# One ring of weights for projection and scan, four turned token tiles, and another order of ScalarE's copies in the scan of a hybrid encoder block

## What is computed

```
h_in = rms_norm(x, norm1_w)
z = h_in @ w_in                              # 2048 x 12,000 columns
z_attn, z_rwkv, z_gate = split(z)
o_attn = dilated attention of z_attn, 3 groups of 8 heads
r, k, v, ... = token_shift_centred(z_rwkv)   # and LoRA inputs of decay, rate, gate
wkv = rwkv7_bidir_scan(r, decay, k, v, kk, iclr)
#   per step: S = S diag(w) + (S (-kk)) (kk*a)^T + v k^T ;  y = S r
o_rwkv = (group_norm(wkv) + bonus) * gate
gates = sigmoid(z_gate + b_gate)
x = x + (gates[0] * (o_attn @ w_branch_attn) + gates[1] * (o_rwkv @ w_branch_rwkv)) @ w_out
h2 = rms_norm(x, norm2_w)
x = x + (silu(h2 @ w_ffn_gate) * (h2 @ w_ffn_up)) @ w_ffn_down
```

## Time and profile before

| | us |
|---|---|
| median of 3 runs (lowest, highest) | 3564.29 (3562.63, 3566.81) |
| profiled execution | 3572.36 |
| its span | 3570.7 |
| PE busy | 3455.4 (97%) |
| POOL / DVE / ACT busy | 1681.8 / 1592.5 / 1113.1 |
| projection, scan, output (from the timeline) | 0 to 1016, 1016 to 1748, 1748 to 3571 |

### The profile page before, as it was taken

One profiled execution on the slowest core, in us unless ns is written; L12 is line 12 of the kernel. 1 busy time (PEld: TensorE's weight loads), 2 busy tenths in 40 slices (PEclk: granted clock), 3 DMA queues, 4 the chain that ended last, 5 costly groups with the idle time before them and its releaser, 6 DMA issues.

```text
span 3570.7 us, 43837 instructions
## 1 busy us (share of the span) xinstructions
PE 3455.4 (97%) x16535; PEld 2800.2 (78%) x16535; DVE 1592.5 (45%) x1894; ACT 1113.1 (31%) x1759; POOL 1681.8 (47%) x1427
## 2 busy tenths in 40 slices
PE   7999999999988999999799999999999999999999
PEld 5777777777767888888568878888888888888887
DVE  4455545555547777776254443320332033203321
ACT  4333324444224544544243232211221122112221
POOL 3433333332318888888275434434444444444443
PEclk8999999999989999999899999999999999999999
DMA  5444444343345455454543423323332333233333
GB/s 179 112 124 132 129 118 148 111 116 92 95 122 129 126 124 130 121 138 104 183 155 110 120 84 104 94 86 105 102 95 85 104 98 102 84 104 94 99 91 104
DMA packets 757676, 406.25 MB, mean 114 GB/s; under 512 B 191694, under 2 KB 718218, under 8 KB 757034
## 3 DMA queue, kind: packets, MB, share of 16 engines
q1 hardware_dynamic: 757546, 404.53, 39.8%
HBM read 345.73 MB, written 58.72 MB: 113 GB/s over the span
## 4 chain that ended last, share of the span: by engine, by line
PE 49%; DVE 1%; ACT 0%; DMA 0%; POOL 0%; issue 0%; SPq 0%; DVEq 0%; ACTq 0%; POOLq 0%
PE f_bank L149 15%; PE f_bank L150 15%; PE f_bank L151 15%; PE f_bank L1856 1%; PE f_bank L1858 1%; PE f_bank L1857 1%; DMA act_plain<-yt 0%; POOL w_lo_b L140 0%; PE f_bank L1865 0%; PE f_bank L1889 0%; DVE hid_plain L2313 0%; ACT w_hi_b L133 0%; PE f_bank L1869 0%; DVE act_rounded L2267 0%; PE f_bank L1972 0%
## 5 line engine op out<-in xcount | busy, mean ns | idle before, releaser
L140 POOL TENSOR_TENSOR w_lo_b<-w_raw_b,w_hi_b 128x2048 fp32r<-128x2048 f32 (+1 forms) x168 | 685.0, 4077 | 924.7 <-ACT w_hi_b L133 924.7
L149 PE MATMUL f_bank<-act_rounded,w_lo_b 128*128 128x512 f32 x1664 | 648.7, 390 | 9.1 <-DVE act_rounded L2267 6.6
L151 PE MATMUL f_bank<-act_rounded,w_hi_b 128*128 128x512 f32 x1664 | 648.1, 389 | 0.0
L150 PE MATMUL f_bank<-act_rounded,w_hi_b 128*128 128x512 f32 x1664 | 648.0, 389 | 0.0
L1254 POOL TENSOR_TENSOR slab_w_rounded<-slab_w_plain,slab_w_hi 128x1024 fp32r<-128x1024 f32 x136 | 327.2, 2407 | 603.5 <-ACT slab_w_hi L1267 603.5
L133 ACT CAST w_hi_b<-w_raw_b 128x2048 fp32r<-128x2048 f32 (+1 forms) x168 | 286.5, 1705 | 838.2 <-PE f_bank L151 827.9
L1546 PE MATMUL slab_ps<-h_hi,slab_w_rounded 128*128 128x512 f32 x1088 | 452.8, 416 | 4.8 <-POOL slab_w_rounded L1254 2.2
L1548 PE MATMUL slab_ps<-h_hi,slab_w_hi 128*128 128x512 f32 x1088 | 427.5, 393 | 0.0
L1547 PE MATMUL slab_ps<-h_lo,slab_w_hi 128*128 128x512 f32 x1088 | 427.4, 393 | 0.0
L149 PEld LDWEIGHTS f_bank<-act_rounded,w_lo_b 128*128 128x128 f32 x1664 | 312.9, 188 | 75.5 <-DVE act_rounded L2267 5.3
L151 PEld LDWEIGHTS f_bank<-act_rounded,w_hi_b 128*128 128x128 f32 x1664 | 312.8, 188 | 65.0
(11 more groups left out here) (347 smaller groups left out, 5271.5 us busy)
## 6 DMA issues: line engine op xcount, KB each, us to landing
slab_w_plain<-in_w_in_dram SPq DMA_DIRECT2D x136, 512.0 KB, 4.1
w_raw_b<-in_w_ffn_gate_dram SPq DMA_DIRECT2D x44, 1024.0 KB, 5.2
w_raw_b<-in_w_ffn_up_dram SPq DMA_DIRECT2D x44, 1024.0 KB, 5.1
w_raw_b<-in_w_ffn_down_dram SPq DMA_DIRECT2D x64, 704.0 KB, 4.4
gate_w_plain<-in_w_in_dram SPq DMA_DIRECT2D x54, 512.0 KB, 4.7
zt<-slab_out SPq DMA_DIRECT2D x65, 256.0 KB, 4.4
w_raw_b<-in_w_out_dram SPq DMA_DIRECT2D x16, 1024.0 KB, 5.6
zt<-lout SPq DMA_DIRECT2D x40, 256.0 KB, 4.6
```

What stands on the lines that cost most here:

```text
L140: pool.tensor_tensor(g.w_lo[n.slot][:, 0:k, :], g.w_raw[n.slot][:, 0:k, :], g.w_hi[n.slot][:, 0:k, :].bitcast(F32), ALU.subtract).then_inc ...
L149: pe.matmul(bank, wl, hi[:, ka, :], start=start and j == 0, stop=False)
L150: pe.matmul(bank, wh, lo[:, ka, :], start=False, stop=False)
L151: ins = pe.matmul(bank, wh, hi[:, ka, :], start=False, stop=stop and j == len(ks) - 1)
```

## The change

1. **Opening.** `x_turned` gets four places instead of two (the third and fourth lie where the slab outputs lie later, so the first slab output waits for their stores). The load of `norm1` moves up behind the first tile of x, and PE turns it after the first tile. ACT takes all four sums of squares first; DVE scales tiles 0 and 1 whole, and of tiles 2 and 3 DVE scales the first half of the channels and ACT the second. PE's first `turn_x` waits for DVE's scaling of all four.
2. **Shared ring.** One ring `ring_w` serves both blocks. The projection already loads the scan's first 4 halves, rounds 3 and makes 2 low parts (on POOL); the scan starts from there.
3. **ScalarE's order in a slot.** `wx` comes before `ta` and `tb`; `st` comes before `akv` and `y` and waits for `yh` itself.

```diff
+RING = 5
+PRE_RAW, PRE_HI, PRE_LO = 4, 3, 2
...
-ACT_SLOT = (("x1", "u"), ("ta", "v"), ("tb", "v"), ("wx", "u"), ("ux", "u"), ("tk", "v"), ("tv", "v"),
-            ("exps", "w"), ("vbd", "w"), ("akv", "v"), ("y", "u"), ("st", "u"))
+ACT_SLOT = (("x1", "u"), ("wx", "u"), ("ta", "v"), ("tb", "v"), ("ux", "u"), ("tk", "v"), ("tv", "v"),
+            ("exps", "w"), ("vbd", "w"), ("st", "u"), ("akv", "v"), ("y", "u"))
...
-                weights(0)
                 load(0)
-                for h in range(1, 4):
-                    weights(h)
...
-                for h in range(3):
-                    high(h)
...
-                for h in range(2):
-                    for q in range(2):
-                        low_part(h, q)
...
-                    if kk == 0:
-                        pe.wait_ge(lo_ready, h + 1)
+                    if kk == 0 and h >= PRE_LO:
+                        pe.wait_ge(lo_ready, h + 1 - PRE_LO)
...
                         if n >= 1:
-                            pe.wait_ge(taken_act, ACT_AT["st" if has_stage("st", n - 1) else "y", n - 1])
+                            pe.wait_ge(taken_act, ACT_AT["y", n - 1])
...
-                    if h >= NH:
+                    if h >= NH + PRE_RAW:
                         return
...
+                    if t == 0:
+                        sp.wait_ge(zeroed, 2)
+                        dst, src = row_loads[0]
+                        sp.dma_start(dst, src).then_inc(norm1_landed, 16)
                     if t == 1:
                         weights(0)
-                sp.wait_ge(zeroed, 2)
-                dst, src = row_loads[0]
-                sp.dma_start(dst, src).then_inc(norm1_landed, 16)
...
-                for h in range(NH):
+                for h in range(NH + PRE_LO):
                     pool.wait_ge(hi_ready, h + 1)
...
-                square_sum(0)
-                square_sum(1)
-                scale(0)
-                square_sum(2)
-                scale(1)
-                square_sum(3)
+                for t in range(TT):
+                    square_sum(t)
                 high(0)
                 scale(2)
-                scale(3)
                 for k in range(KD):
                     high_h(k)
+                    if k == 1:
+                        scale(3)
...
-                    if t >= 2:
-                        dve.wait_ge(x_kept[t % 2], 16)
...
+                            if n == Q0:
+                                dve.wait_ge(x_kept[2], 16)
+                                dve.wait_ge(x_kept[3], 16)
...
                         if k == 0:
-                            pe.wait_ge(scaled_act, t + 1)
-                        if k == KD // 2:
                             pe.wait_ge(scaled_dve, t + 1)
+                        if k == KD // 2 and t >= 2:
+                            pe.wait_ge(scaled_act, t - 1)
```

More of the change, by code:

```diff
@@ L363, in phase_scan @@
         d_landed = [sem(f"d_landed{i}") for i in range(2)]
-        w_landed = [sem(f"gate_w_landed{i}") for i in range(RAW_RING)]
+        w_landed = [sem(f"gate_w_landed{i}") for i in range(RING)]
         hi_ready, lo_ready, w_used, gate_taken = sem("gate_hi_ready"), sem("gate_lo_ready"), sem("gate_w_used"), sem("gate_taken")
@@ L612, in low_part @@
                 def low_part(h, q):
[L613 to L614 removed]
+                    if q == 0 and h >= PRE_HI:
+                        dve.wait_ge(hi_ready, h + 1 - PRE_HI)
                     r = slice(q * (KH // 2), (q + 1) * (KH // 2))
@@ L1029, in phase_project @@
         sem = nc.alloc_semaphore
-        w_lo, w_raw = two_faced(nc, ctx, "slab_w", [P, RING * KH, P])
-        w_hi = sb("slab_w_hi", [P, (RING - 1) * KH, P], F32R)
+        w_lo, w_raw, w_hi = g.ring_lo, g.ring_raw, g.ring_hi
+        with ExitStack() as early:
+            x_late = [early.enter_context(nc.sbuf_tensor(f"x_turned{i}", [P, KD, P], F32)) for i in (2, 3)]
         out = [sb(f"slab_out{i}", [P, SEQ]) for i in range(NOUT)]
@@ L1038, in phase_project @@
             x_tok = eb("x_tok", [P, TT, D_MODEL])
-            x_turned = [eb(f"x_turned{i}", [P, KD, P]) for i in range(2)]
+            x_turned = [eb(f"x_turned{i}", [P, KD, P]) for i in range(2)] + x_late
             lora = eb("lora", [P, 3, SEQ])
@@ L1228, in _ @@
                     sp.wait_ge(out_stored[i], 16 * len(range(Q0 + i, N_SLOT, NOUT)))
-                for i in range(2):
-                    sp.wait_ge(x_kept[i], 16 * (TT // 2))
+                for t in range(TT):
+                    sp.wait_ge(x_kept[t], 16)
+                for h in range(NH + PRE_RAW - RING, NH + PRE_RAW):
+                    sp.wait_ge(w_landed[h % RING], 16 * (h // RING + 1))
                 sp.wait_ge(kk_stored, 16 * NPAIR)
@@ L1399, in _ @@
                     dve.scalar_tensor_tensor(out=v, in0=v, scalar=-1.0, in1=v, op0=ALU.mult, op1=ALU.max).then_inc(dist_abs, 1)
-                for t in range(TT):
-                    if t < 3:
-                        for b in range(4):
-                            keep(t, b)
-                            if b == 1:
-                                mean_square(t)
-                    else:
-                        mean_square(t)
-                    if t >= 1:
-                        scale(t - 1)
-                    if t == 2:
-                        dve.wait_ge(par_turned, 1)
-                        dve.tensor_copy(param(g, "norm1", 0, KD), heads_ps[:, 0:KD]).then_inc(par_ready, 1)
+                for b in range(4):
+                    keep(0, b)
+                    if b == 1:
+                        mean_square(0)
+                dve.wait_ge(par_turned, 1)
+                dve.tensor_copy(param(g, "norm1", 0, KD), heads_ps[:, 0:KD]).then_inc(par_ready, 1)
+                scale(0)
+                for b in range(4):
+                    keep(1, b)
+                    if b == 1:
+                        mean_square(1)
+                for b in range(4):
+                    keep(2, b)
+                    if b == 1:
+                        mean_square(2)
+                scale(1)
+                scale(2)
+                mean_square(3)
                 scale(3)
```

51 lines of the change are left out of this document (29 added, 22 removed).

## The result

| | before | after |
|---|---|---|
| median of the runs beside each other (lowest, highest) | 3565.55 (3562.63, 3574.11) | 3531.49 (3529.55, 3532.02) |
| ratio (95% interval) | | 0.9902 (0.9890 to 0.9914) |
| profiled execution, its span | 3572.36, 3570.7 | 3531.09, 3529.4 |

The changed kernel takes 3531.49 us against 3530.3 predicted: 34.1 us less in the medians. The two profiled executions lie 41.3 apart. One number of the kernel's description has to be put right: the projection has 68 slabs, 67 of them after slab 0, not 80.

The account below looks back on a forecast made before the run. PE, busy for 97% of the span, was taken as the bound. Opening 9.5, boundary 7.5 and scan 17 sum to 34 us: 3572.36 becomes 3538.4, less 8.07 to the median, 3530.3; range 3518 to 3545.

Parts of the forecast that it names:

- Opening, 9.5: Opening: without DVE's wait on a store, PE's transpose at 32.45 comes at 22.9; 9.5 us gained, bounds 6 to 12.
- Boundary, 7.5: Projection to scan: first weights ready early, so PE's whole scan start moves 7.5 us earlier, bounds 4 to 8.
- Scan, 17: Scan slots: both `w_bd` waits (26.4 us) go, less what becomes late next; 17 us gained, bounds 8 and 23.5.
- the 23.5 that I had as the cap: Scan: the gain can't exceed POOL's 25.0 us of gaps less a handover each, 23.5 us.
- (a): Scan: PE's waits for DVE's bonus input grow by 0.5 in each of some 8 cases, 4 us back.
- (c): Scan: the way behind the inverse has 1.3 to 2 us of slack; PE stops at two or three pairs, some 5 us.
- The 17.6 behind my 17: Scan: gain left at the last of 14 pairs; POOL beside a denser DVE costs another 0.5 to 1.
- 8.07: Whole kernel: the profiled execution was 8.07 us above the median of the runs shown, so 3538.4 becomes 3530.3.
- A: Rival, scan: the inverse keeps the scan, each new `x1` wait paid in full; scan 8, sum 25, 3539; chance 0.2.
- B: Rival: DVE's last scaling before POOL's low part (0.75), POOL's gaps all used; sum 43, 3521; chance 0.13.
- C: Rival, scan: denser DVE stretches POOL's inverses from 38.7 to 42.5 us; slower, 3572; chance 0.02.

Follow-up runs that it names:

- short inverses: Changed kernel with the last four of each inverse's 30 elimination steps left out, so part of the computation is changed: 3518.68 us, ratio 0.9861.
- the loads on ACT's queue: Changed kernel with each scan unit's six loads issued by ScalarE at the end of its slot instead of by SP: 3571.73 us, ratio 1.0010.
- W's spread alone: Kernel before with only W's spread moved right behind x1's copy, the state's spread still last: 3550.94 us, ratio 0.9954.
- the slots alone: Kernel before with only the scan's edits: ScalarE's order in a slot and the three waits belonging to it: 3546.75 us, ratio 0.9940.

## Why the prediction was right, point by point

- **Opening, 9.5: right.** 10.1 to 10.2 in the profiles, 10.0 in the medians. The block is complete at 21.73 where I had 22.9. What was off is my count of DVE's queue, in small steps: it was through with the third tile's copies at 16.2 (I had 16.9), the scalings of tile 1 and half of tile 2 took 1.94 (1.4 + 0.75), and the last one began at 18.85 (20.1). The 2.70 for the last one, taken from the earlier trace rows, came as 2.82.
- **Boundary, 7.5: right.** 7.8 in the profile, 6.0 alone in the medians (2.9 to 9.3). The idle time of 4.0, the half clock behind it, the operands 1 us ahead of PE and `cum` 11 us after the last slab matmul came as written; only the 3.80 at `x1` shrank, to 2.84.
- **Scan, 17: right in size, and partly for other reasons.** 18.4 in the profile, 21.0 alone. That POOL's gaps cap it holds: 25.0 became 3.5, and POOL's first to last inverse fell by 20.4, against the 23.5 that I had as the cap. The terms behind it were off. (a) The bonus waits did not grow by 4: 8.7 became 8.2. (c) I had PE stop for the inverse at two or three pairs, some 5 us; it stopped at one, for 3.41 us (`x1` at 1668.57), where before there was one stop of 0.5 beside that of unit 0. What I did not list is how it reaches PE by another way: it also holds up SP's one queue, and with it the next unit's loads, `decays`, `qg` and so `yh` (6.7 us), and `x3` grew by 4. The rows of the slot at 1360 show this way; both with short inverses and with the loads on ACT's queue the waits at `yh` were gone, which fits it, though no run tests it free of other effects. The 17.6 behind my 17 came from a walk through 14 pairs of slots of which the prediction shows only the rules, so it can't be compared pair by pair.
- **The balance of the 18.4.** Waits fell by 40.2 - 26.2 = 14.0. Half clock grew from 10.3 to 20.5 us, which costs 5.1. The rest fell by 9.5: a wait costs more than the idle time of its row. The rows show where. In slot 20 of the kernel before, the gate matmul ahead of the wait starts at 1525.36 and the stage on `w_bd` at 1526.32, 0.96 later, of which the row calls 0.57 idle. Without a wait the same two follow each other in 0.23 (1368.17 and 1368.40 in the kernel after). So the wait cost 0.73 there, 0.16 more than shown, and the eight matmuls behind it took 1.16 instead of 1.05:

```profile
1525.36 0.39 PE L744 MATMUL gbank<-h_hi,gate_w_hi 128*128 128x512 f32 x1
```

  The 0.16 is the part of the row's 0.39 us in which the next matmul already runs when there is no wait. At `ts` it is the same: 0.17, and 0.66 instead of 0.60 for the four matmuls. In the scan PE's waits above 0.15 us fell from 60 to 19; 9.5 over 41 is 0.23 each, against 0.27 and 0.23 in these two examples (0.22 with W's spread alone, where 23 went; 0.19 with the slots alone, 38). I had neither the half clock (-5.1) nor this surcharge (+9.5) in my sum, and new waits came to 12.4 us (6.7 at `yh`, 4.1 at `x3`, 1.9 more at `x1`) where I had 9. The three errors nearly cancel, so that the scan's term fits within 1.4 us is partly luck.
- **From the profiled run to the median.** I took 8.07 off, by three runs. By twenty runs of before it is 3572.36 - 3567.74 = 4.6. The long half clock in slab 66 is in that gap. With 4.6 the same 34 us give 3533.8, so that the forecast came within 1.2 us of the measured time is luck as well.
- **Rivals.** A is ruled out for the slots alone (16.8 to 26.4 by their interval). B's two conditions: POOL's gaps were used up but for 3.5, DVE's last scaling stayed slow, and making it fast brought nothing that the medians show. C: inverses took 38.7 before and (623.5 - 3.5) / 16 = 38.75 after; a denser DVE did not stretch them.

## What to carry to other kernels

Ask of every wait that you remove which chain runs beside it with how much idle time: here a chain of sixteen inverses on POOL with 25 us of gaps capped 26 us of waits, and the second of two moves gave 2 us by the trace (4 in the medians) for its 10.8. A queue that issues everything in one order is a resource of its own: twice a transfer that had nothing to do with the edit stood at the head of SP's queue and passed the delay on. And when a wait goes but the time stays, look for it a stage or two further on at the same engine: the bonus sum's wait fell from 15.1 to 0.9 us, and that at `x3` grew from 2.1 to 14.9.

## What the runs showed of the hardware that I had not expected

- The clock fell at short stops. The four longest stops of PE in the scan after are 2.48 us before 1066.61, 2.84 before 1084.96, 2.22 before 1373.25 and 3.41 before 1668.57; during or up to 1 us behind them it fell to half (2.4 to 1.2 GHz), for 3.4, 6.8, 3.4 and 6.8 us:

```profile
1085.00:1090.00 5.00, 5.00 (x20) 4.71 (x21) 1.22 (x3) 0.59 (x1) 4.29 (x10) 0.50 0.58 123
...
1375.00:1380.00 5.00, 5.00 (x29) 4.73 (x28) 4.93 (x7) 1.21 (x4) 4.45 (x8) 0.74 0.02 4
...
1670.00:1675.00 5.00, 5.00 (x20) 4.41 (x19) 0.69 (x1) 0.59 (x1) 0.00 (x0) 0.54 0.31 87
```

  So a few long waits have a price beside their idle time: the scan after has 14.0 us less of waits than before but twice as much half clock (20.5 us against 10.3).
- In slab 66, behind 1.1 us of idle time, the same code ran at half clock for 20.5 us in one profile and some 10 in another; in three of the variants it didn't at all. Between the profiles this stretch alone makes up to 9.4 us (21.1 to 30.5). How much it makes in the runs without a profile isn't shown.
- Six DMA issues cost ACT 4.8 us and SP 3.9 us of their own time, 0.4 to 1.4 each.
- DVE's 128x256 operations on two SBUF tiles took 0.40 to 0.43 while POOL was idle (the four of `decays` of unit 0 behind `cum`, from 1007.48) and 0.76 to 0.83 beside POOL's inverse (from 1369.37):

```profile
1007.91 0.43 DVE L687 TENSOR_TENSOR ex<-cum,sw_in 128x256 f32<-128x256 f32 x1
...
1370.17 0.77 DVE L687 TENSOR_TENSOR ex<-cum,sw_in 128x256 f32<-128x256 f32 x1
```
